# All sixteen state tiles in one scan with a doubling carry, weight loads of one piece each, a head on VectorE in two steps

## The reference

```python
def second_block(x, ...):
    h = rms_norm_2(x, attn_norm_g[i])
    proj = h @ w_in[i] + b_in[i]
    q, k, v, u, gate_attn, gate_ssm = jnp.split(proj, SPLIT_POINTS, axis=-1)
    attn = sliding_window_attention(q, k, v, attn_sinks[i])      # 16 heads of 64
    y = s5_ssm(u, ...)                                           # 32 groups of 64 complex states
    y_val, y_gate = jnp.split(gelu(y) @ w_glu[i] + b_glu[i], 2, axis=-1)
    ssm = y_val * sigmoid(y_gate)
    merged = (sigmoid(gate_attn) * (attn @ w_branch_attn[i])
              + sigmoid(gate_ssm) * (ssm @ w_branch_ssm[i]))
    x = x + merged @ w_out[i]
    ...                                                          # then a gated feed-forward block

def s5_ssm(...):
    bu = einsum(bb, ug)                    # complex, (batch, position, group, state)
    # x[t] = a * x[t-1] + bu[t], complex, over the 256 positions
    _, _, xs_re, xs_im = lax.associative_scan(combine, (a_re_t, a_im_t, bu_re, bu_im), axis=1)
    y = einsum(c_re, xs_re) - einsum(c_im, xs_im) + d_skip * ug
```

## Time and profile before

| | |
|---|---|
| runs (3) | median 2974.09 us, 2971.7 to 2974.18 |
| profiled execution | 2972.43 us, its span 2971.2 us |
| TensorE busy in the span | 2900.2 us, 98% |
| VectorE, ScalarE, GpSimd busy | 1672.1, 1323.6, 288.5 us |
| mean granted clock of TensorE | 0.993 of full speed |

### The profile page before, as it was taken

One profiled execution on the slowest core, in us unless ns is written; L12 is line 12 of the kernel. 1 busy time (PEld: TensorE's weight loads), 2 busy tenths in 40 slices (PEclk: granted clock), 3 DMA queues, 4 the chain that ended last, 5 costly groups with the idle time before them and its releaser, 6 DMA issues.

```text
span 2971.2 us, 32087 instructions
## 1 busy us (share of the span) xinstructions
PE 2900.2 (98%) x13201; PEld 2374.1 (80%) x13201; DVE 1672.1 (56%) x1935; ACT 1323.6 (45%) x1638; POOL 288.5 (10%) x369
## 2 busy tenths in 40 slices
PE   8999999999999999999999999996999999999998
PEld 6888887888888888888888887675788888888886
DVE  4464655555555455455555567664755656656444
ACT  5444445444444444444444454443544444444443
POOL 0000000000000000000000069396100000000000
PEclk9999999999999999999999999998999999999999
DMA  6545454555555555555555554453555555555553
GB/s 230 198 169 186 156 189 141 170 198 196 186 185 184 197 186 186 196 184 187 189 194 199 185 167 149 135 181 108 186 182 196 172 196 184 184 186 189 191 198 128
DMA packets 278174, 536.72 MB, mean 181 GB/s; under 512 B 17217, under 2 KB 19709, under 8 KB 278029
## 3 DMA queue, kind: packets, MB, share of 16 engines
q1 hardware_dynamic: 266400, 528.52, 52.7%
q10 hardware_dynamic: 11629, 6.17, 0.8%
HBM read 532.55 MB, written 2.10 MB: 180 GB/s over the span
## 4 chain that ended last, share of the span: by engine, by line
PE 88%; POOL 5%; DVE 4%; ACT 2%; issue 1%; DMA 1%; ACTq 0%; DVEq 0%
PE panels L549 28%; PE panels L551 28%; PE panels L550 28%; PE side L567 2%; DVE weights_lo L1589 2%; POOL scan_step L419 1%; POOL ssm_states L424 1%; POOL scan_step L416 1%; POOL ssm_states L441 1%; POOL ssm_states L423 1%; POOL ssm_scratch L439 1%; ACT weights_hi L1079 0%; POOL merged L452 0%; PE side L746 0%; DMA x<-in_x 0%
## 5 line engine op out<-in xcount | busy, mean ns | idle before, releaser
L1589 DVE TENSOR_TENSOR weights_lo<-weights,weights_hi 128x1024 fp32r<-128x1024 f32 (+1 forms) x1032 | 1262.6, 1229 | 1009.6 <-ACT weights_hi L1079 1004.8
L1079 ACT ACTIVATE weights_hi<-weights 128x1024 fp32r<-128x1024 f32 (+1 forms) x1032 | 1064.4, 1035 | 1153.6 <-PE panels L551 1144.3
L549 PE MATMUL panels<-weights_hi,xT_hi 128*128 128x512 f32 (+1 forms) x2752 | 1086.7, 395 | 2.0 <-DVE xT_lo L1637 1.8
L551 PE MATMUL panels<-weights_hi,xT_lo 128*128 128x512 f32 (+1 forms) x2752 | 1071.9, 389 | 0.0
L550 PE MATMUL panels<-weights_lo,xT_hi 128*128 128x512 f32 (+1 forms) x2752 | 1071.0, 389 | 0.0
L549 PEld LDWEIGHTS panels<-weights_hi,xT_hi 128*128 128x128 f32 x2752 | 518.3, 188 | 114.0 <-issue 8.2
L551 PEld LDWEIGHTS panels<-weights_hi,xT_lo 128*128 128x128 f32 x2752 | 517.8, 188 | 108.6
L550 PEld LDWEIGHTS panels<-weights_lo,xT_hi 128*128 128x128 f32 x2752 | 518.6, 188 | 102.0 <-issue 0.2
L549 PE MATMUL panels<-weights_hi,hiddenT_hi 128*128 128x512 f32 x704 | 275.8, 392 | 3.5 <-DVE weights_lo L1589 2.0
L551 PE MATMUL panels<-weights_hi,hiddenT_lo 128*128 128x512 f32 x704 | 274.4, 390 | 0.0
L550 PE MATMUL panels<-weights_lo,hiddenT_hi 128*128 128x512 f32 x704 | 274.3, 390 | 0.0
(11 more groups left out here) (305 smaller groups left out, 2110.9 us busy)
## 6 DMA issues: line engine op xcount, KB each, us to landing
weights<-in_w_in SPq DMA_DIRECT2D x164, 1024.0 KB, 4.9
weights<-in_w_up SPq DMA_DIRECT2D x88, 1024.0 KB, 4.9
weights<-in_w_ffn_gate SPq DMA_DIRECT2D x44, 1024.0 KB, 5.0
weights<-in_w_ffn_up SPq DMA_DIRECT2D x44, 1024.0 KB, 5.0
weights<-in_w_out SPq DMA_DIRECT2D x32, 1024.0 KB, 5.0
weights<-in_w_ffn_down SPq DMA_DIRECT2D x32, 1024.0 KB, 5.0
weights<-in_w_down SPq DMA_DIRECT2D x32, 1024.0 KB, 5.0
weights<-in_w_ffn_down SPq DMA_DIRECT2D x16, 768.0 KB, 4.2
```

Of the source, the lines that this page charges most:

```text
L549: pe.matmul(acc, a, wh, start=k0 + k == 0, stop=False)
L551: inst = pe.matmul(acc, b, wh, start=False, stop=k0 + k == total - 1)
L1079: self.act.activation(self.m.HI[:, g % PIECES, 0:n], raw, ACT.Copy).then_inc(self.ev["hi_split"])
L1589: self.dve.tensor_tensor(m.LO[:, ring, 0:n], raw, m.HI[:, ring, 0:n].bitcast(F32), ALU.subtract).then_inc(self.ev["lo_split"])
```

## The change

It has four parts.

1. `weights` has four slots of one piece (two slices) instead of four of two pieces; each piece has a DMA of its own, and the load of piece g waits for the `weights_lo` of piece g-4. There are 1016 loads instead of 516. The last twelve slices of a down projection are no longer cut 2, 1, 2, 1: a panel there has 22 pieces of two instead of 24.
2. The 16 KB of each partition that this frees hold all sixteen state tiles at once: `ssm_states` beside `q2` makes all of them (`dense` is now an extra step after every second piece, before it was every fourth), and GpSimd does one scan over all, with instructions on twice as many elements.
3. The carry between blocks is done by doubling: four calls of `advance` over distances 1, 2, 4 and 8, with the powers a^16, a^32, a^64 and a^128, instead of fifteen calls in each half. VectorE makes the powers in `ssm_powers` with 21 more small instructions, in one more step.
4. The interlude is gone. `ssm_output` does the outputs of all sixteen tiles from the first piece of `gate_ssm[3]` on, and GELU and its `lo` part follow there. VectorE's part of a head is cut in two steps: `head_norm` (the sum, the reciprocal, the division) comes after the next piece's `weights_lo`. This holds for both attentions.

```diff
-        self.RAW = sb("weights", [P, 4, CK * PANEL], 0)
+        self.RAW = sb("weights", [P, SLOTS, 2 * PANEL], 0)
...
-    def load_chunk(self, c, pan, k0, nk):
-        slot = c % SLOTS
-        if c >= SLOTS:
-            self.sp.wait_ge(self.ev["lo_split"], 2 * (c - SLOTS) + 2)
+    def load_piece(self, g, pan, k0, size):
+        slot = g % SLOTS
+        if g >= SLOTS:
+            self.sp.wait_ge(self.ev["lo_split"], g - SLOTS + 1)
...
-        self.scan(0)
-        self.scan(1)
+        self.scan()
...
-        pool.wait_ge(ev["states_in"], nt * (half + 1))
+        pool.wait_ge(ev["states_in"], ST)
...
-            pool.wait_ge(ev["pool_step"], same_ready)
+            pool.wait_ge(ev["pool_step"], self.steps)
...
         for j in range(BLK - 1):
             advance(X5[:, :, :, :, j], X5[:, :, :, :, j + 1], 20, NB)
-        for b in range(NB - 1):
-            advance(X5[:, :, :, b:b + 1, BLK - 1], X5[:, :, :, b + 1:b + 2, BLK - 1], 24, 1)
+        for d, coef in ((1, 24), (2, 0), (4, 4), (8, 8)):
+            advance(X5[:, :, :, 0:NB - d, BLK - 1], X5[:, :, :, d:NB, BLK - 1], coef, NB - d)
...
-        side.add(self.ssm_first_half(), self.ssm_outputs_setup())
+        side.add(self.ssm_states(), self.ssm_outputs_setup())
         for pan in plan.q2:
-            self.panel(pan, X, side, dense=True)
+            self.panel(pan, X, side, dense=2)
...
         for pan in plan.gate_attn + plan.gate_ssm:
+            if pan is plan.gate_ssm[3]:
+                side.add(self.ssm_output())
             self.panel(pan, X, side)
...
         for p in range(3):
-            if p == 2:
-                side.add(self.ssm_end())
             self.panel(plan.branch_attn[p], (m.OH2, m.OL2), side)
...
-            if interlude and h == MIDWAY:
-                yield from interlude
...
+        def head_norm(h):
+            b = h % 2
+            pr = ptile[:, b, :]
             dve.wait_ge(ev["exped"], h + 1)
...
         head_scores(0)
+        head_norm(0)
         yield
         for h in range(heads + 1):
             if h + 1 < heads:
                 head_scores(h + 1)
             if h:
                 head_out(h - 1)
             yield
+            if h + 1 < heads:
+                head_norm(h + 1)
             if h < heads:
                 yield
...
+        for at in (0, 4, 8):
+            step(dve.tensor_tensor(sv[:, 17, :], sv[:, re, :], sv[:, re, :], ALU.mult))
+            step(dve.tensor_tensor(sv[:, 18, :], sv[:, im, :], sv[:, im, :], ALU.mult))
+            step(dve.tensor_tensor(sv[:, at, :], sv[:, 17, :], sv[:, 18, :], ALU.subtract))
+            step(dve.tensor_tensor(sv[:, 17, :], sv[:, re, :], sv[:, im, :], ALU.mult))
+            step(dve.tensor_copy(sv[:, at + 1, :], sv[:, at, :]))
+            step(dve.tensor_scalar(sv[:, at + 2, :], sv[:, 17, :], -2.0, None, ALU.mult))
+            inst = dve.tensor_scalar(sv[:, at + 3, :], sv[:, 17, :], 2.0, None, ALU.mult)
```

More of the change, by code:

```diff
@@ L324, in program @@
         sp.wait_ge(ev["loaded_x_load0"], 16)
[L325 to L326 removed]
+        for g, (pan, k0, size) in enumerate(self.plan.pieces):
+            self.load_piece(g, pan, k0, size)
         for h in range(2):
@@ L715, in a_down, with attention @@
         yield
-    def attention(self, which, heads, scores, values, ptile, ptT, dh, interlude=None):
+    def attention(self, which, heads, scores, values, ptile, ptT, dh):
         pe, m = self.pe, self.m
@@ L928, in ssm_output @@
             yield
-    def ssm_halves(self):
-        yield from self.ssm_output(0)
-        yield from self.ssm_input(1)
-    def ssm_end(self):
-        yield from self.ssm_output(1)
-        self.pe.wait_ge(self.ev["gel_lo"], 1)
+        for _ in range(3):
+            yield
+        pe.wait_ge(ev["gel_lo"], 1)
     def attention2(self):
@@ L1279, in a_down, with attention @@
         act.activation(m.ADT[:, :], m.SIDE[0:RANK, 0, 0:S], ACT.Copy).then_inc(ev["adt_ready"])
-    def attention(self, which, heads, out, scale, ptile, ptT, dh, sink=None, interlude=None):
+    def attention(self, which, heads, out, scale, ptile, ptT, dh, sink=None):
         act, m = self.act, self.m
@@ L1431, in ssm_input, with ssm_output @@
                 yield
-    def ssm_halves(self):
-        yield
-        yield
-        yield from self.ssm_input(1)
-    def ssm_end(self):
+    def ssm_output(self):
         act, m, ev = self.act, self.m, self.ev
-        yield
-        yield
+        for _ in range(4):
+            yield
         act.wait_ge(ev["y_ready"], 4)
@@ L1834, in a_down, with attention @@
             yield
-    def attention(self, which, heads, out, dist, slope, scale, ptile, dh, sink=None, interlude=None):
+    def attention(self, which, heads, out, dist, slope, scale, ptile, dh, sink=None):
         dve, m = self.dve, self.m
@@ L2075, in ssm_first_half, with ssm_output @@
             yield
-        for _ in range(4):
+        for _ in range(8):
             yield
-    def ssm_output(self, half):
+    def ssm_output(self):
         dve, m, ev = self.dve, self.m, self.ev
-        for u in (2 * half, 2 * half + 1):
+        for u in range(4):
             dve.wait_ge(ev["y_done"], u + 1)
@@ L2085, in ssm_output @@
             yield
-    def ssm_halves(self):
-        yield from self.ssm_output(0)
-        for _ in range(4):
-            yield
-    def ssm_end(self):
-        dve, m, ev = self.dve, self.m, self.ev
-        yield from self.ssm_output(1)
         dve.wait_ge(ev["gel_hi"], 1)
```

203 lines of the change are left out of this document (88 added, 115 removed).

## The result

The changed kernel takes 2994.03 us (median of 4 runs, 2992.63 to 2995.4), the kernel before 2973.44 in the same comparison: a ratio of 1.0068, 95% interval 1.0056 to 1.008. It is slower by 20.6 us, where 9 us less were forecast.

A forecast was written before the change was run, and what follows sets the result against it. TensorE, busy 98%, bounds the kernel; its large wait is 22.1 us for GpSimd's last correction. -32.6 + 6 + 6 + 3 + 3 + 2.3 + 2.3 + 1 = -9.0 us gives 2963.4, 2965 on the median's scale; range 2949 to 2980.

The forecast's parts named there:

- Corrections beside heads: Attention heads under GpSimd's corrections: 10.4 us of VectorE each with the cut, four heads, +6 us, bounds 0 and 12.
- the port: SBUF port pair that VectorE and GpSimd take in turn, each for its whole instruction, so they hold each other up.
- `kv2` and the first score: Beside `kv2`, VectorE waits for longer GpSimd instructions, 2.1 us per `weights_lo` for 1.6: +6 us, bounds 0 and 10.
- Gate panels after the heads: After the heads, a panel's `weights_lo` and evacuation take VectorE 20 to 24 us against 21.7: +3 us, bounds 0 and 6.
- Half speed behind short stops: TensorE's lower clock behind the stalls of heads and panels: +3 us, as behind the first stage before.
- Loads: Loads of one piece are mostly covered; pieces of one slice in `glu` and `branch_ssm` cost +1 us, bounds 0 and 4.
- cover of 8.4 us: Time from asking for a piece's load to ScalarE's need of it, against a landing of 3.5 us.
- Rival 3: Late loads: VectorE's delays over 4.9 us delay half-size loads, 0.15 us at some 120 panels, +18, 2983 us; chance 0.06.
- The scan: GpSimd's one scan starts at 1745, doublings end at 1910, corrections at 1988; outputs beside `gate_ssm[3]` wait 0 us.
- Rival 4: Scan ends much later than wanted, at 2010; TensorE stands 16 us in `gate_ssm[3]`: +8, 2982 us; chance 0.08.
- the first down projection: VectorE's 21 small instructions for the scan's powers make TensorE wait there: +2.3 us, bounds 0 and 5.
- rival 2: Port delays in `kv2`, heads and outputs eat the gain: no change midway, chance 0.17; extreme +10, 2984 us, chance 0.06.

The follow-up runs named there:

- the repaired head: Changed kernel with ScalarE's exponentials behind the copy of the next piece and the sink's sum moved from VectorE to ScalarE: 2957.2 us, ratio 0.9942.
- short steps: Changed kernel with the repaired head, and each of GpSimd's nineteen advances in two halves of eight state tiles: 2971.1 us, ratio 0.9989.

## Why the prediction was wrong

**The step that failed** is this one, in "Corrections beside heads": "The cut in two takes the wait of 1.24 us out of VectorE's head and lets two `weights_lo` no longer follow each other". The order of VectorE's instructions says that; ScalarE's order was not laid beside it. The cut put a copy of ScalarE's between the maxima and VectorE's next instruction, and that copy stands behind the exponentials. Taking just this out gave 20.4 us of the 29 by which the forecast missed. Against one step the cut costs 7.7 us; the other 12.7 are what the cut can bring once ScalarE's order fits it. The second half of the sentence failed with it: 2 × 0.5 us for `weights_lo` that no longer follow each other are named, left out of the 10.4, and mostly not there (2.55 and 2.83 us, 2.86 each before). The same step made the heads under the scan's steps longer: the forecast gave them 7.9 us each, the eight from 1815.3 to 1895.4 took 10.0; with ScalarE's order mended 8.1 was the rule there.

**The term that was mis-sized** is the port. The forecast gave 18 us to what GpSimd holds up (6 in `kv2`, 6 under the corrections, 3 in the gate panels, 3 for half speed). The run without a scan says 58.4, of which 20.4 are the order of ScalarE's queue above. In parts:
- `kv2` and the first score: idle time of 3.8 us in 1780 to 1812, the first distances at 1815.3, 8 us later than without a scan (1807.2). Place right, size within the bounds.
- Under the corrections stood five heads and part of a sixth (8.8 us), not four, and the five took 13.5 us each, not 10.4. Heads that are late stay under the corrections, and make themselves later.
- Gate panels after the heads: nothing, since no head was done before the corrections were.
- Half speed behind short stops: 16.8 us, not 3. TensorE's clock in 1812 to 1975 was 0.87, and 0.97 with the exponentials behind the copy.

Without GpSimd's share the forecast is 2965 - 18 = 2947, the run 2935.6: 11.4 us the other way. The stretches of the kernel before show 7 of them: the two scans cost it 39.7 us in 1734 to 2066 and not the 32.6 that were counted. Left out were 2.1 us idle in 1734 to 1812 (a number that the prediction itself gives), 2.7 in 1812 to 1838 (1.0 idle, 1.7 by a clock of 0.93), 1.3 idle in 1875 to 1996, and some 1 of half speed behind the long wait. The other 4 stay open. The two misses, 40.4 less 11.4, make the 29.

**Loads:** the forecast's 1 us is 8 us by itself, of which 4.5 in `q2` and `kv2` and 1.5 beside `glu` are placed. The cover of 8.4 us was worked out for whole pieces, and `kv2` has pieces of half the time. Rival 3 named the right resource and the wrong place. The rule of the Trainium skill ("DMA: Bandwidth & Descriptors", "Bandwidth"), DMAs of 1 MiB or more, was set aside for a row of 390 GB/s; its direction held here, by 8 us, though what the run shows is late landings beside short pieces and not a lack of bandwidth. The runs don't separate size from number of DMAs.

**The scan:** start 1748.8 (1745), end of the doublings 1897.2 (1910), end 1968.7 (1988, bounds 1965 to 2010), 69 us before TensorE came for the outputs. Rival 4 didn't come. With the repaired head, and the scan's instructions as long as forecast, the scan ended at 1984.3 and TensorE asked at 2000.0, still without a wait; the wait of 30.2 us came when short steps moved the scan's end to 2010. The forecast took start, end and heads one by one, while they move together.

**A reading that was wrong:** 1.28 us for a `weights_lo` "where GpSimd's instructions are short". GpSimd's instructions in 1970 to 1997 are the second scan's steps on 256 elements, as in 1923 to 1955, where it took 1.65. What differs is VectorE: no head stands there, and it is idle before most of them (1.54 us before the one at 1978.18, of 1.22 us). GpSimd's addition at 1978.35 then took 1.80 us, the one before it 0.91. So the engine that comes second waits, and an instruction after idle time paid little. The 1.28 went only into the cover of the loads, where it changes nothing.

**Right:** the 22.1 us went. TensorE waited 3.7 us in two waits for `weights_lo` in the first down projection (2.0 before; forecast, with its share, +2.3). In `q2`, 1.0 us for u and 0.6 for the c matrices, of which 1.1 stood there before. Nothing was seen of the first attention's new cut.

**The rivals:** rival 2, "the gain is eaten by the port", is the one that came, by more than its extreme of 2984, though the 6 us that it gave to the outputs did not. Its bound for the heads (12 us) was too low, since it kept the saved 1.24 us and four heads. Its condition, that the corrections begin before head 9, was the right question: the ninth head's distances stand at 1895.4, the corrections begin at 1897.2.

## What to carry to other kernels

A wait is only out of an engine's way if the instruction put in front of it depends on nothing behind that wait: when one engine's steps are cut, lay the queues of all engines of the chain side by side, and follow what the moved instruction itself waits for. Where two engines hold each other up one instruction at a time, count the turns of a round and not busy time: short instructions on one side and fewer on the other are the two remedies, and a tiny instruction can cost a whole turn. Short instructions make the side that runs them longer (here 30 us), so look at who waits for its end. And a term that says "covered by this margin" needs the margin worked out again for each other term that moves either end.

## What the runs showed of the hardware

- VectorE's and GpSimd's instructions lock into a round of whole turns. A head took 13.5, 11.6 or 9.7 us beside 6, 5 or 4 instructions of 900 elements, and 10.7 us beside 8 of 450. The Trainium skill ("SBUF — State Buffer", "Who interferes with whom") has a lock held for the whole instruction; the trace agrees.
- An addition on 128x2 elements took 1.75 us there and 0.15 without the scan, where the reciprocal of as many took 0.17 in both. `weights_lo` took 2.55 to 2.83 us, and 1.23 without the scan. `row_max`, a reduction, took 0.61 us for two in both. The same page says that a reduction never takes the shared ports and that two operands from SBUF do; the rows agree.
- GpSimd's steps and carries with twice as many instructions of half the size took 178 us (1746.9 to 1925.2) instead of 148 (1748.8 to 1897.2), beside the same attention.
- The doubling carry, with four calls for fifteen, was only some 8 us shorter. The fifteen took 25 us, 1.7 each, where one that met nobody took 1.15 (1816.95 to 1818.10): most of these small instructions ran between two of VectorE's, so there was less to save than their number says.
